# Decoder layer on eight cores: the first loads of tiles and weights issued in another order

## The reference

```
h = rms_norm(x, norm_mix);  proj = h @ w_in
q, k, v, u, g_a, g_p = split(proj)              # 512, 512, 512, 512, 1024, 1024
q = partial_rope(rms_norm(q, q_norm));  k = partial_rope(rms_norm(k, k_norm))
o_attn = moba_attention(q, k, v)                # 8 heads; own block of 256 and the best 3 past blocks
o_pool = multiscale_pool(u, w_pool_grp, pool_scale)   # causal window means less the token
x = x + (sigmoid(g_a) * (o_attn @ w_up_attn) + sigmoid(g_p) * (o_pool @ w_up_pool)) @ w_out
x = x + relu(rms_norm(x, norm_mlp) @ w_ff1)^2 @ w_ff2
```

## Time and profile before

| | |
|---|---|
| median of 3 runs | 940.35 us (939.48 to 942.74) |
| profiled execution, its own time | 939.31 us |
| its span (slowest core, core 3) | 938.0 us |
| spans of the 8 cores | 932.2 to 938.0 us |
| TensorE busy in the span | 901.4 us (96%) |
| VectorE, ScalarE, GpSimd busy | 457.4, 368.8, 113.2 us |
| transfers issued from GpSimd, from SyncE | 40.28 MB, 36.75 MB |

### The profile page before, as it was taken

The page is one execution under the profiler, slowest core; times in us unless marked ns, Lnnn a source line. Parts: engine busy times, 40 slices in busy tenths (PEclk is TensorE's granted clock), DMA queues, the critical chain, the costliest instruction groups (busy, mean ns, idle before and its releaser), DMA issues.

```text
span 938.0 us, 17381 instructions; the slowest of 8 cores (932.2 to 938.0 us)
## 1 busy us (share of the span) xinstructions
PE 901.4 (96%) x5724; PEld 461.7 (49%) x5724; DVE 457.4 (49%) x858; ACT 368.8 (39%) x730; POOL 113.2 (12%) x201
## 2 busy tenths in 40 slices
PE   2899998899999999999999999999999999999998
PEld 1444454567777764444444444444444444444444
DVE  2788875656423234334774444444444443444444
ACT  2677545798999962221006234031111221111220
POOL 4212211221000000100101111001110111000000
PEclk9999999999999999999999999999999999999999
DMA  8963342234443444993997434014330333201113
GB/s 199 216 147 88 62 130 52 53 42 83 81 72 58 70 79 107 192 201 80 171 135 117 51 51 55 14 24 56 47 55 1 44 47 57 35 1 68 68 68 157
DMA packets 66341, 78.12 MB, mean 83 GB/s; under 512 B 35984, under 2 KB 54672, under 8 KB 66000
## 3 DMA queue, kind: packets, MB, share of 16 engines
q0 software_dynamic: 25056, 40.28, 29.3%
q1 hardware_dynamic: 41200, 36.75, 16.3%
HBM read 98.41 MB, written 8.39 MB: 114 GB/s over the span
## 4 chain that ended last, share of the span: by engine, by line
PE 89%; DMA 4%; DVE 2%; issue 2%; ACT 2%; DVEq 0%; POOL 0%; ACTq 0%; POOLq 0%; SPq 0%
PE bank L1372 24%; PE bank L1343 24%; PE bank L1013 11%; PE bank L433 9%; PE bank L907 6%; PE bank L1243 6%; PE bank L945 3%; PE bank L1027 3%; PE bank L1032 3%; DMA raw<-x 2%; DMA raw<-w_slice 1%; DMA raw<-w_qkvu 1%; PE bank L487 1%; PE bank L520 1%; DVE raw L461 0%
## 5 line engine op out<-in xcount | busy, mean ns | idle before, releaser
L1350 ACT ACTIVATE raw<-bank 128x512 f32<-128x512 f32 x128 | 76.4, 597 | 375.6 <-PE bank L1343 316.9
L1372 PE MATMUL bank<-raw 128*128 128x512 bf16 (+1 forms) x1032 | 223.2, 377 | 0.0
L1343 PE MATMUL bank<-raw 128*128 128x512 bf16 x1024 | 223.1, 379 | 0.0
L1372 PEld LDWEIGHTS bank<-raw 128*128 128x128 bf16 x1032 | 101.0, 98 | 120.2
L1343 PEld LDWEIGHTS bank<-raw 128*128 128x128 bf16 x1024 | 100.2, 98 | 120.8
L1352 DVE SCALAR_TENSOR_TENSOR raw<-bank,raw 128x512 bf16<-128x512 f32 x128 | 88.6, 692 | 140.6 <-ACT raw L1350 140.6
L914 ACT ACTIVATE raw<-bank 128x512 bf16<-128x512 f32 (+1 forms) x288 | 146.1, 591 | 21.7 <-PE bank L945 20.6
L1380 DVE SCALAR_TENSOR_TENSOR raw<-bank,raw 128x512 f32<-128x512 f32 x129 | 96.3, 747 | 112.5 <-PE bank L1372 112.0
L433 PE MATMUL bank<-raw 128*128 128x512 bf16 x512 | 122.8, 390 | 9.6 <-ACT raw L372 4.0
L1013 PE MATMUL bank<-raw 128*128 128x512 bf16 x512 | 122.5, 379 | 0.7 <-DMA raw<-w_slice 0.7
L907 PE MATMUL bank<-raw 128*128 128x256 bf16 x576 | 98.4, 266 | 2.4 <-ACT raw L914 1.9
(11 more groups left out here) (91 smaller groups left out, 578.5 us busy)
## 6 DMA issues: line engine op xcount, KB each, us to landing
raw<-x SPq DMA_DIRECT2D x32, 512.0 KB, 6.9
raw<-w_ff POOLq DMA_DIRECT2D x64, 256.0 KB, 4.0
raw<-w_slice POOLq DMA_DIRECT2D x22, 640.0 KB, 7.8
out<-raw SPq DMA_DIRECT2D x15, 512.0 KB, 2.6
raw<-w_qkvu POOLq DMA_DIRECT2D x8, 512.0 KB, 12.9
raw<-raw SPq DMA_DIRECT2D x2, 1024.0 KB, 4.8
raw<-w_out POOLq DMA_DIRECT2D x4, 512.0 KB, 13.7
raw<-c_ind POOLq DMA_DIRECT2D x4, 256.0 KB, 4.3
```

Of the source, the lines that this page charges most:

```text
L1343: t.group("pe", [lambda e, c=c, j=j, bk=bk: e.matmul(bank_f(bk), lhsT=ffw1[s][:, c, j * 128:(j + 1) * 128], rhs=hT[:, c, tg * 512:(tg + 1) ...
L1350: t.op("act", lambda e, bk=bk, si_=si_: e.activation(out=sqz[si_], in_=bank_f(bk), func=AF.Square), reads=hb[bk], writes=[b_sqz[si_]])
L1372: t.group("pe", [lambda e, j=j, bk=bk, i=i, c0_=c0_, c1_=c1_, n_=n_: e.matmul(bank_f(bk)[:, 0:n_], lhsT=a1T[ab][:, j, i * 128:(i + 1) * 12 ...
```

## The change

Tile 1 is issued from SyncE directly behind the gain vector, ahead of SyncE's wait for the first K half; tile 2 and the rest stay behind that wait. The V weights are issued from GpSimd behind `pool_setup` without a wait for tile 1. The U load waits for slot 2 where it waited for slot 1, and depends on the multiply of tile 3 where it depended on that of tile 2; the Q load's earliest time is 25 where it was 26. The arrival times and the times at which GpSimd and SyncE become free are new numbers, so the planner makes the order of the stage anew.

```diff
--- before.py
+++ after.py
@@ -629,16 +629,15 @@
             t.dma("pool", ident_b, c_ident_d, writes=[b_ident])
             t.dma("sp", gmix_bc, gmix_vec_d, writes=[b_gmix_bc])
             load_w(CG_K)
+            p0_load(1)
             pool_setup()
+            load_w(CG_V)
             t.wait_written("sp", b_wqkvu[CG_K][0])
-            p0_load(1)
             p0_load(2)
             t.dma("sp", small_c, c_small_d, writes=[b_small, b_gcq, b_gck])
             t.dma("sp", gv_qk, c_gv_d.partition_broadcast(128), writes=[b_gv])
             t.dma("sp", rope_t, c_rope_d.rearrange("p (t n) -> p t n", t=NT), writes=[b_rope])
             p0_load(3)
-            t.wait_written("pool", b_xslot[1])
-            load_w(CG_V)
 
         first_loads()
 
@@ -646,8 +645,8 @@
             t.wait_written("pool", b_xslot[sl])
             load_w(cg)
 
-        W_AT = {CG_K: 15.0, CG_V: 30.0, CG_Q: 43.0, CG_U: 54.0}
-        X_AT = [4.7, 16.3, 18.6, 23.0]
+        W_AT = {CG_K: 14.8, CG_V: 26.0, CG_Q: 38.0, CG_U: 48.0}
+        X_AT = [4.9, 11.5, 17.5, 21.5]
         ji_of = {jb: ji for ji, jb in enumerate(jobs)}
         k_ev_t, q_ev_t, hev, ujob = {}, {}, {}, {}
         NT_PE = 9
@@ -746,8 +745,8 @@
         last_root = [k_ for k_ in tasks if k_.name == "root"][-1]
         pj_of = [k_ for k_ in tasks if k_.name.startswith("pj_")]
         by_job = dict(zip(jobs, pj_of))
-        add("wq", 4.0, [("pool", 2.0, lambda: load_w_after(CG_Q, 0))], deps=[muls[1]], after=26.0)
-        add("wu", 8.0, [("pool", 2.0, lambda: load_w_after(CG_U, 1))], deps=[muls[2]], after=34.0)
+        add("wq", 4.0, [("pool", 2.0, lambda: load_w_after(CG_Q, 0))], deps=[muls[1]], after=25.0)
+        add("wu", 8.0, [("pool", 2.0, lambda: load_w_after(CG_U, 2))], deps=[muls[3]], after=34.0)
         add("band_ld", 12.0, [("pool", 1.0, lambda: t.dma("pool", band, c_band_d, writes=[b_band]))], after=40.0)
         add("wg_ld", 20.0, [("pool", 1.0, lambda: t.dma("pool", wgT_f, w_grpT_d, writes=[b_wgTf]))], after=60.0)
         add("tri", 30.0, [("pool", 1.5, late_setup)], after=80.0)
@@ -767,7 +766,7 @@
 
         LAT = 0.2
         free_at = {n_: {i: 0.0 for i in v_} for n_, v_ in pools.items()}
-        eng_free = {"pe": 0.0, "act": 0.0, "dve": 0.0, "pool": 20.0, "sp": 22.0}
+        eng_free = {"pe": 0.0, "act": 0.0, "dve": 0.0, "pool": 17.0, "sp": 21.0}
         INF = 1e18
         left = list(tasks)
         order = []
```

## The result

The changed kernel takes 947.91 us (median of 7 runs, 946.62 to 951.57), the kernel before 940.61 beside it (7 runs, 939.48 to 943.47). The ratio is 1.0089 with a 95% interval of 1.0073 to 1.0106: 7.3 us slower, where 937.0 was forecast and 943.0 was the upper end of the range. In some executions the cores of a die run longer at a lower granted clock; all times here are medians of the other executions. The profiled execution took 947.65 us, with a span of 946.6 on core 2, the slowest. From attention on little changed: the span goes on for 785.8 us behind the first attention matmul, where before it went on for 784.9 (core 3).

The account below looks back on a forecast made before the run. TensorE was taken as full from 45 us, held earlier by waits for loads. 939.31 less 3.3 gives 936.0; the runs' median lies 1.04 higher: 937.0, own range 935.2 to 939.0, overall 933.5 to 943.0.

Parts of the forecast that it names:

- the premise of its first part: Projection stage: TensorE works 101.50 of 105 us from 45 to 150, so time won before 45 us is kept.
- the sum: Profiled 939.31 us less a gain of 3.3 gives 936.0; the runs' median lies 1.04 higher, so 937.0.
- the later tiles: Tile 4, still releasing Q, and tile 5, needing only tile 1's multiply, and those behind: costed at nothing.
- the slack of 4.8 us of tile 6: Tile 6's transposes came 4.8 us after the 3.3 us it needs past landing; this would cover a 3.3 us lead.
- its own sign of being wrong: Wrong if TensorE has clearly more than 3.5 us of holes from 45 to 150, among other signs.
- Tile 1, K, V: First loads: tile 1 lands at 12.9, 5.5 us sooner; K's halves at 13.6 and 16.9; V near 28, 4.9 sooner.
- what K pays: GpSimd's queue slows to 103 GB/s beside tile 1, so K's halves land 1.4 us later.
- Tiles 2 and 3: With V beside them, tile 2 lands at 20.9 and tile 3 at 27.8, or about 23 at the early end.
- The pair of V0 and K3: V job of tile 0 and K job of tile 3: end at 31.6 to 35.3, gaining 1.4 to 5.1, middle 3.3.
- U: U load now waits for tile 6 in slot 2; costed at nothing, as tile 6 is issued no later.
- The rival of a held GpSimd: GpSimd stands at the U load for a late tile 6, losing 3.9 us: 944.2 us, chance 0.13.
- The transfers only change places: Rival: tile 1 and V come early, tiles 2, 3 and K pay it all; 940.4 us give or take 1.5, chance 0.23.

Follow-up runs that it names:

- e12: Kernel before with tile 1 issued ahead of SyncE's wait and V held until tile 2 has landed, old order: 939.5 us, ratio 1.0006.
- e1: The changed kernel's new loads with the old planner numbers, so the old order: 941.8 us, ratio 1.0024.
- e2: The kernel before's old loads with the new planner numbers, so the new order: 947.11 us, ratio 1.0080.
- e13: Changed kernel, every engine's order kept, U's issue held until tile 9 has landed: 947.2 us, ratio 1.0083.
- e17: Changed kernel, every engine's order kept, U's issue held until tile 11 has landed: 950.8 us, ratio 1.0116.
- e14: Changed kernel, same order, with three of the four rotary steps that VectorE does for a tile left out: 947.14 and 948.44 us.
- e5: Changed kernel, planner taking squares of tiles 7 to 15 as ready 9 us after their planned transfer end, not 1.5: 935.16 us, ratio 0.9953.
- e10: Old loads with the new planner numbers, squares of tiles 7 to 15 planned 9 us after transfer end: 933.98 us, ratio 0.9947.
- e6: Kernel before, old loads and numbers, squares of tiles 7 to 15 planned 7.5 us after transfer end: 933.97 us, ratio 0.9940.
- e9: Changed kernel, squares of tiles 7 to 15 planned 6 us after transfer end, not 1.5: 951.54 us, ratio 1.0134.
- e7: Changed kernel, planner given the arrivals its own trace showed for tiles 1 to 3 and the weights: 954.24 us, ratio 1.0156.
- e8: Kernel before with only the new assumed arrival times of tiles 0 to 3 in the planner: 943.9 us, ratio 1.0040.
- e16: Kernel before with only the new free times of GpSimd and SyncE and the new Q and U tasks: 944.1 us, ratio 1.0043.

## Why the prediction was wrong, point by point

**The step that failed** is the premise of its first part, "time lost before 45 us is lost for good, and time won there is kept if TensorE stays as full behind it", whose condition was taken as given. The order made anew has no term in the sum beyond 45 us, and the later tiles have one of nothing ("I cost these at nothing"), as the slack of 4.8 us of tile 6 was taken to cover them. TensorE didn't stay as full: its idle time from 45 to 100 us went from 2.90 to 8.55 us, and its matmuls there took 239 ns in place of 227. The cover failed at tile 8, for which ScalarE waited 4.39 us (before, 0.55). The first half of the premise is neither shown nor refuted: the slowest cores of both kernels had done 64 projection matmuls by 45 us. That TensorE works 101.50 of 105 us holds only for the old order. The prediction gave its own sign of being wrong, "clearly more than 3.5 us of holes between 45 and 150", and that is what came, but no rival had this mechanism and none had a price for it.

Step by step:

- *Tile 1, K, V.* Tile 1 landed at 12.2 (12.9 forecast), K's halves at 14.05 and about 17.0 (13.6, 16.9). V was issued at 11.41 and was there at about 25.3, sooner than the 28 forecast. The step on what K pays was right.
- *Tiles 2 and 3.* Tile 3 landed at 27.4 (27.8). Tile 2 was mis-sized: 24.6 in place of 20.9. It was issued at 14.1, as the chain of waits of core 2 shows, and none of its packets moved before 17.5. The queues in 12 to 15, 15 to 17.5 and 17.5 to 20 us:

```profile
2.24 11.81 DMA raw<-w_qkvu
14.12 10.48 DMA raw<-x
```

```profile
q0 software_dynamic: 128, 0.47, 100.4%
...
q0 software_dynamic: 119, 0.43, 104.5%
...
q0 software_dynamic: 90, 0.31, 79.1%
q1 hardware_dynamic: 51, 0.21, 24.7%
```

  The sum had SyncE's queue at 118 GB/s from 16 us on; it moved nothing up to 17.5, and then 0.21 MB in 2.5 us, 84 GB/s. That V came sooner than forecast is the other side of it.
- *The pair of V0 and K3* was one group with a second V job (34.63, 24 matmuls). By ScalarE's list its first two jobs are V jobs, the second evicted at 38.34, and K3 is the last and ends at 39.97; the pair ended at 36.71 before, and 31.6 to 35.3 was forecast. Tile 2's lateness is the 5.86 us hole ahead of it. The lead of tile 1 was spent there, and e12, without that lateness, still gains nothing.
- *U* was issued at 39.92 without a hold. The rival of a held GpSimd did not occur; its time, 944.2, was nearer than the forecast for another reason.
- *The transfers only change places* fits the early part best: it had no gain and no loss, give or take 1.5 us, and in the old order the loads cost 2.3 us (e1). The Trainium skill's rule in "DMA: Bandwidth & Descriptors", section "Issuing engines are not separate DMA queues", that transfers run on the same 16 engines and interleave whichever engine started them, agrees with there being no gain; the interleaving doesn't show from 14.1 to 17.5 us, where GpSimd's queue moved everything.

**What is shown, and what stays open.** Shown: the order and not the loads carries the loss (e2). The stretch from 45 to 100 us does 22 jobs where it did 26. Two kinds of holes of TensorE make the difference: those behind waits for tiles at the squares, which hold evictions (54.07, and in e13 and e17 at other tiles), and those that all eight cores have with one length (1.42 us, in e2, e14 and e17 too, and 1.93 us, in these and in e13); and matmuls ran at the lower clock behind the longest. With 9 us (e5, e10) or 7.5 us (e6) for tiles 7 to 15 the planner makes orders that do 26 or 27 jobs there; with 6 us (e9) it does not. Open: which dependency makes the holes that all cores share, and so why e9's order, and e7's with holes of 0.78 and 1.98 us on every core, are slow. The planner's own plan put 26 or 27 jobs between 45 and 100 us in the kernel before and in e5 and e6, and 23 to 25 in the changed kernel, e7, e8, e9 and e16; that goes along with the times, but it was not varied by itself, so it is a description and not a cause.

## What to carry to other kernels

When numbers of a planner change, the whole order is a new kernel: price the order over the stage, not only the loads at its start, and run the new loads in the old order and the reverse first. In a fixed order an instruction that waits for a late transfer holds all behind it, so put such instructions behind work that needs nothing. Here a later arrival in the planner did that at 7.5 and 9 us and did harm at 6; the spacing that the trace shows (5 us, not 2.6) was not tried, so each such number is a trial to be measured. Compare the holes of all cores: one that has the same length on every core points to the order, one that differs from core to core to what the cores wait for. A full engine in a trace shows that this order fills it, not that another order will.

## What the runs showed of the hardware that was not expected

A transfer issued from SyncE at 14.1 us, while GpSimd's queue stood at 100 to 105%, moved no packet until 17.5 and landed 10.5 us after its issue; with V held back until it had landed (e12) the same tile took 4.7 us. In the kernel before both queues moved side by side when both were long full, so the share is no constant of the pair. And the granted clock, 1.00 from 20 to 40 us before, read 0.74 there after, with TensorE idle for 5.86 us inside, and again 0.50 from 56 to 58 us, behind the hole of 2.96:

```profile
20.00:40.00 20.00, 13.16 (x64) 6.20 (x63) 11.38 (x24) 9.92 (x22) 5.99 (x11) 0.74 0.81 206
```
